# Stick-breaking attention with the queries on the partitions and the suffix sums on VectorE

## What is computed

```
z           = (q @ k.T) * scale                     # per head, queries x keys
past        = s_idx < t_idx
log_beta    = log_sigmoid(z)
log_1mb     = where(past, log_sigmoid(-z), 0)
between     = reverse_cumsum(log_1mb, over keys) - log_1mb
a           = where(past, exp(log_beta + between), 0)
out         = a @ v
```

## Time and profile before

| | us |
|---|---|
| median of 3 runs (1226.33 to 1226.4) | 1226.34 |
| profiled execution | 1226.2 |
| its span | 1224.4 |
| PE busy | 1204.7 (98%) |
| PE weight loads busy | 1053.1 (86%) |
| DVE busy | 772.5 (63%) |
| ACT busy | 609.4 (50%) |
| DMA, bytes moved | 219 MB at 179 GB/s |

### The profile page before, as it was taken

One profiled execution on the slowest core, in us unless ns is written; L12 is line 12 of the kernel. 1 busy time (PEld: TensorE's weight loads), 2 busy tenths in 40 slices (PEclk: granted clock), 3 DMA queues, 4 the chain that ended last, 5 costly groups with the idle time before them and its releaser, 6 DMA issues.

```text
span 1224.4 us, 17707 instructions
## 1 busy us (share of the span) xinstructions
PE 1204.7 (98%) x7176; PEld 1053.1 (86%) x7176; DVE 772.5 (63%) x883; ACT 609.4 (50%) x711; POOL 3.5 (0%) x10
## 2 busy tenths in 40 slices
PE   7999999999999999999999999999999999999997
PEld 6999987888888799899888789999988878899995
DVE  5676966474555665555458687555575868755555
ACT  6565555555444454444257545444435654544441
POOL 0000000000000000000000000000000000000000
PEclk9999999999999999999999999999999999999999
DMA  7654243543655355554364445545436444564540
GB/s 255 207 210 166 104 173 139 205 172 138 218 207 183 126 206 207 176 202 173 135 236 178 147 173 206 207 172 206 171 137 242 168 150 172 199 214 172 206 171 34
DMA packets 34490, 219.25 MB, mean 179 GB/s; under 512 B 4080, under 2 KB 6144, under 8 KB 9088
## 3 DMA queue, kind: packets, MB, share of 16 engines
q1 hardware_dynamic: 33792, 216.31, 49.6%
q0 software_dynamic: 640, 2.11, 0.5%
HBM read 217.34 MB, written 1.06 MB: 178 GB/s over the span
## 4 chain that ended last, share of the span: by engine, by line
PE 92%; DVE 6%; ACT 1%; issue 1%; DMA 0%; SPq 0%; DVEq 0%; ACTq 0%
PE gps L1440 33%; PE gps L1479 9%; PE gps L1487 9%; PE gps L1480 9%; PE aps L1479 7%; PE aps L1480 7%; PE aps L1487 7%; DVE w_lo L788 1%; PE aps L1602 1%; PE aps L1505 1%; DVE rs L919 1%; ACT w_hi L341 1%; DVE B L929 1%; PE aps L1641 1%; DVE B L870 1%
## 5 line engine op out<-in xcount | busy, mean ns | idle before, releaser
L788 DVE TENSOR_TENSOR w_lo<-raw,w_hi 128x2048 fp32r<-128x2048 f32 x194 | 444.2, 2291 | 260.4 <-ACT w_hi L341 259.9
L341 ACT ACTIVATE w_hi<-raw 128x2048 fp32r<-128x2048 f32 x194 | 370.5, 1911 | 208.0 <-PE aps L1487 104.1
L1440 PE MATMUL gps<-R_hi,w_hi 128*128 128x256 f32 x672 | 175.8, 283 | 0.0
L1440 PE MATMUL gps<-R_hi,w_lo 128*128 128x256 f32 x672 | 175.7, 283 | 0.0
L1479 PE MATMUL aps<-w_hi,Q_hi 128*128 128x512 f32 x416 | 162.2, 390 | 0.5 <-DVE Q_lo L1201 0.5
L1480 PE MATMUL aps<-w_lo,Q_hi 128*128 128x512 f32 x416 | 162.2, 390 | 0.0
L1440 PE MATMUL gps<-R_lo,w_hi 128*128 128x256 f32 x672 | 135.4, 283 | 0.0
L1440 PEld LDWEIGHTS gps<-R_hi,w_lo 128*128 128x128 f32 x672 | 128.9, 192 | 0.8
L1440 PEld LDWEIGHTS gps<-R_hi,w_hi 128*128 128x128 f32 x672 | 128.8, 192 | 0.8
L1479 PE MATMUL gps<-w_hi,H_hi 128*128 128x512 f32 x288 | 114.8, 399 | 0.0
L1480 PE MATMUL gps<-w_lo,H_hi 128*128 128x512 f32 x288 | 112.5, 390 | 0.0
(11 more groups left out here) (241 smaller groups left out, 1670.6 us busy)
## 6 DMA issues: line engine op xcount, KB each, us to landing
raw<-w SPq DMA_DIRECT2D x194, 1024.0 KB, 4.8
B<-rows SPq DMA_DIRECT2D x4, 1024.0 KB, 5.6
raw<-w SPq DMA_DIRECT2D x8, 256.0 KB, 6.0
B<-turns POOLq DMA_DIRECT2D x4, 512.0 KB, 7.7
B<-x_t SPq DMA_DIRECT2D x4, 256.0 KB, 5.4
B<-mem_t SPq DMA_DIRECT2D x1, 1024.0 KB, 8.9
B<-x SPq DMA_DIRECT2D x1, 1024.0 KB, 6.8
out<-B SPq DMA_DIRECT2D x4, 256.0 KB, 2.0
```

Source lines behind the costliest of these rows:

```text
L341: act.activation(w_hi[:, ring(l), :], raw[:, raw_slot(l), :], ACT.Copy)\
L788: dve.tensor_tensor(w_lo[:, ring(l), :], raw[:, raw_slot(l), :], w_hi[:, ring(l), :].bitcast(F32), ALU.subtract)\
L1440: return pe.matmul(gps[:, bank_, nt * T:(nt + 1) * T], w[:, r, c:c + P], op[:, k, :], start=start, stop=stop, skip_group_check=True)
```

## The change

The scores are made with the queries on the partitions, with the same numbers of columns. The blocks of a head are now (queries 0, keys 0), (queries 1, keys 0) and (queries 1, keys 1). The suffix sum runs along a row, so it is a backward scan on DVE, one for each head of the pair; the constant `keep` is one except at the last key of each of the two query groups, where it is zero and starts the sum anew. The masks are no longer multiplied in behind softplus and exp. A mask of 0 and -3e38 is added to the two diagonal blocks of the scores as DVE copies them from PSUM to spb, and ACT copies the third block. Softplus works on soft, z stays in spb. The weights come out of exp with queries on the partitions, so PE transposes six blocks of 128x128 per pair and ACT copies them from PSUM to a new tile `sb_pt`, from which the values product reads.

The order changes too. Even slot: PE has values and scores; ACT sb_out, the copy of the third block, a wait for the mask, Abs, Exp, Ln; DVE sb_out and the mask. Odd slot: PE has the transposes of the pair before, behind its half; ACT the copy of the transposed weights of the pair before, then exp; DVE sum, scans and subtraction. The weight splits stand behind this work, in every slot.

```diff
             def sb_softplus(i):
+                b = spb[:, i % 2, :, :]
                 act.wait_ge(s["sb_z"], i + 1)
                 if i >= 2:
-                    act.wait_ge(s["sb_o"], i - 1)
-                b = spb[:, i % 2, :, :]
-                st.mark(act.activation(b, aps[:, 0:2, 0:384], ACT.Abs))
+                    act.wait_ge(s["sb_t"], i - 1)
+                act.activation(b[:, :, 128:256], aps[:, 0:2, 128:256], ACT.Copy).then_inc(s["sb_full"], 1)
+                act.wait_ge(s["sb_past"], i + 1)
+                if i >= 1:
+                    act.wait_ge(s["sb_arg"], i)
+                st.mark(act.activation(soft[:, :, :], b, ACT.Abs))
                 st.settle()
-                st.mark(act.activation(b, b, ACT.Exp, scale=-1.0))
+                st.mark(act.activation(soft[:, :, :], soft[:, :, :], ACT.Exp, scale=-1.0))
                 st.settle()
-                act.activation(b, b, ACT.Ln, bias=one_col).then_inc(s["sb_sp"], 1)
+                act.activation(soft[:, :, :], soft[:, :, :], ACT.Ln, bias=one_col).then_inc(s["sb_sp"], 1)
...
+            def sb_copy(i):
+                act.wait_ge(s["sb_t"], i + 1)
+                if i >= 1:
+                    act.wait_ge(s["sb_o"], i)
+                act.activation(sb_pt, aps[:, 2:4, 0:384], ACT.Copy).then_inc(s["sb_pt"], 1)
...
-                if SB0 <= h <= SB0 + 18 and h % 2 == 0:
+                if SB0 <= h <= SB0 + 18:
                     t = (h - SB0) // 2
-                    if t >= 2:
-                        sb_out(t - 2)
-                    if t < SB_PAIRS:
-                        sb_softplus(t)
-                    if 1 <= t <= SB_PAIRS:
-                        sb_exp(t - 1)
+                    if h % 2 == 0:
+                        if t >= 2:
+                            sb_out(t - 2)
+                        if t < SB_PAIRS:
+                            sb_softplus(t)
+                    elif t < SB_PAIRS:
+                        if t >= 1:
+                            sb_copy(t - 1)
+                        sb_exp(t)
+                    else:
+                        sb_copy(t - 1)
                 if h + 4 < FFN1 + 2:
                     split(0, h + 4)
...
-            def sb_parts(i):
-                b, z = spb[:, i % 2, :, :], aps[:, 0:2, 0:384]
-                dve.wait_ge(s["sb_sp"], i + 1)
-                if i >= 1:
-                    dve.wait_ge(s["sb_t"], i)
-
-                st.mark(dve.scalar_tensor_tensor(soft[:, :, :], z, 0.0, b, ALU.max, ALU.add))
-                st.settle()
-                mask_diagonals(soft, s["sb_soft"])
-
-                dve.scalar_tensor_tensor(b, z, 0.0, b, ALU.min, ALU.subtract).then_inc(s["sb_lb"], 1)
+            def sb_masked(i):
+                b = spb[:, i % 2, :, :].rearrange("p h (c n) -> p h c n", c=3)
+                z = aps[:, 0:2, 0:384].rearrange("p h (c n) -> p h c n", c=3)
+                dve.wait_ge(s["sb_full"], i + 1)
+                if i >= 2:
+                    dve.wait_ge(s["sb_t"], i - 1)
+                dve.tensor_tensor(b[:, :, 0:3:2, :], z[:, :, 0:3:2, :],
+                                  past.unsqueeze(1).unsqueeze(1).to_broadcast([P, 2, 2, P]), ALU.add)\
+                   .then_inc(s["sb_past"], 1)
 
             def sb_arg(i):
                 b = spb[:, i % 2, :, :]
-                dve.wait_ge(s["sb_t"], i + 1)
-                dve.wait_ge(s["sb_lb"], i + 1)
-                dve.tensor_tensor(b, b, aps[:, 2:4, 0:384], ALU.subtract).then_inc(s["sb_arg"], 1)
-
-            def sb_mask(i):
-                dve.wait_ge(s["sb_e"], i + 1)
-                mask_diagonals(spb[:, i % 2, :, :], s["sb_a"])
+                dve.wait_ge(s["sb_sp"], i + 1)
+                dve.scalar_tensor_tensor(soft[:, :, :], b, 0.0, soft[:, :, :], ALU.max, ALU.add)\
+                   .then_inc(s["sb_sum"], 1)
+                dve.wait_ge(s["sb_sum"], i + 1)
+                for hh in range(2):
+                    ins = dve.tensor_tensor_scan(soft[:, hh, ::-1], keep[:, ::-1], soft[:, hh, ::-1], 0.0,
+                                                 ALU.mult, ALU.add)
+                ins.then_inc(s["sb_suffix"], 1)
+                dve.wait_ge(s["sb_suffix"], i + 1)
+                dve.tensor_tensor(b, b, soft[:, :, :], ALU.subtract).then_inc(s["sb_arg"], 1)
...
-                if SB0 <= h <= SB0 + 18 and h % 2 == 0:
+                if SB0 <= h <= SB0 + 18:
                     t = (h - SB0) // 2
-                    if t >= 2:
-                        sb_out(t - 2)
-                    if 1 <= t <= SB_PAIRS:
-                        sb_arg(t - 1)
-                    if t < SB_PAIRS:
-                        sb_parts(t)
-                    if 1 <= t <= SB_PAIRS:
-                        sb_mask(t - 1)
+                    if h % 2 == 0:
+                        if t >= 2:
+                            sb_out(t - 2)
+                        if t < SB_PAIRS:
+                            sb_masked(t)
+                    elif t < SB_PAIRS:
+                        sb_arg(t)
...
             def sb_scores(i):
                 if i >= 1:
-                    pe.wait_ge(s["sb_lb"], i)
+                    pe.wait_ge(s["sb_past"], i)
                 for hh in range(2):
                     q, k = qs[64 * hh:64 * hh + 64, i, :], ks[64 * hh:64 * hh + 64, i, :]
-                    pe.matmul(aps[:, hh, 0:256], k[:, 0:128], q, start=True, stop=True)
-                    ins = pe.matmul(aps[:, hh, 256:384], k[:, 128:256], q[:, 128:256],
-                                    start=True, stop=True)
+                    pe.matmul(aps[:, hh, 0:128], q[:, 0:128], k[:, 0:128], start=True, stop=False,
+                              skip_group_check=True)
+                    ins = pe.matmul(aps[:, hh, 128:384], q[:, 128:256], k, start=False, stop=True,
+                                    skip_group_check=True)
                 ins.then_inc(s["sb_z"], 1)
 
-            def sb_between(i):
-
-                pe.wait_ge(s["sb_soft"], i + 1)
+            def sb_transpose(i):
+
+                pe.wait_ge(s["sb_e"], i + 1)
                 if i >= 1:
-                    pe.wait_ge(s["sb_arg"], i)
+                    pe.wait_ge(s["sb_pt"], i)
                 for hh in range(2):
-                    pe.matmul(aps[:, 2 + hh, 0:384], gt, soft[:, hh, :], start=True, stop=False)
-                    ins = pe.matmul(aps[:, 2 + hh, 128:256], ones, soft[:, hh, 256:384],
-                                    start=False, stop=True)
+                    for j in range(3):
+                        ins = pe.transpose(aps[:, 2 + hh, j * P:(j + 1) * P],
+                                           spb[:, i % 2, hh, j * P:(j + 1) * P], ident)
                 ins.then_inc(s["sb_t"], 1)
 
             def sb_values(i):
-                pe.wait_ge(s["sb_a"], i + 1)
+                pe.wait_ge(s["sb_pt"], i + 1)
...
-                    if 1 <= t <= SB_PAIRS:
-                        sb_between(t - 1)
+                if SB0 + 3 <= h <= SB0 + 17 and h % 2:
+                    sb_transpose((h - SB0 - 3) // 2)
```

More of the change, by code:

```diff
@@ L53 @@
 N_MLP, N_END, N_LN = 0, 1, 2
-C_ID, C_GT, C_LE, C_ONE, C_PAST, CONSTS1 = 0, 128, 256, 384, 512, 640
+C_ID, C_PAST, C_KEEP, C_ONE, CONSTS1 = 0, 128, 256, 384, 640
 C_COS, C_SIN, C_DECAY, C_CAUSAL, CONSTS2 = 0, 128, 384, 1408, 1792
@@ L103, in build @@
         small = sb("small", [P, 4, 16])
-        ident, gt = cst[:, C_ID:C_ID + P], cst[:, C_GT:C_GT + P]
-        le_one = cst[:, C_LE:C_LE + 2 * P]
-        le, ones = cst[:, C_LE:C_LE + P], cst[:, C_ONE:C_ONE + P]
+        ident, ones = cst[:, C_ID:C_ID + P], cst[:, C_ONE:C_ONE + P]
         past = cst[:, C_PAST:C_PAST + P]
+        keep = cst[:, C_KEEP:C_KEEP + 384]
         one_col = cst[:, C_ONE:C_ONE + 1]
@@ L153, in build @@
         bias = B6[:, :, :].rearrange("p h (t k) -> p h t k", t=2)
+        sb_pt = B7[:, 0:3, :].rearrange("p a t -> p (a t)").rearrange("p (h n) -> p h n", h=2)
         fl = spb[:, 0, :, :]
@@ L168, in build @@
             staged_free conv_y cv_hi cv_lo
-            sb_z sb_sp sb_soft sb_lb sb_t sb_arg sb_e sb_a sb_o sb_ohi sb_olo
+            sb_z sb_past sb_full sb_sp sb_sum sb_suffix sb_arg sb_e sb_t sb_pt sb_o sb_ohi sb_olo
             hd_sq hd_var hd_log hd_r hd_z hd_tr hd_out
@@ L1014, in ffn @@
                     split_gates(n)
[L1016 to L1023, removed]
             def sb_out(i):
@@ L1612, in sb_values @@
                     c = (2 * i + hh) * 64
-                    a = spb[:, i % 2, hh, :]
+                    a = sb_pt[:, hh, :]
                     out = gps[64 * hh:64 * hh + 64, 3, :]
@@ L1623, in turn_heads @@
                 if n == 0:
-                    pe.wait_ge(s["sb_lb"], SB_PAIRS)
+                    pe.wait_ge(s["sb_past"], SB_PAIRS)
                 else:
@@ L1950, in shape_constants @@
     c1[:, C_ID:C_ID + P] = np.eye(P)
[L1951 to L1954, removed]
+    c1[:, C_PAST:C_PAST + P] = np.where(i[None, :] < i[:, None], 0.0, -3.0e38)
```

(2 more changed lines are left out.)

## The result

| | before | after |
|---|---|---|
| median, us | 1226.37 (1226.33 to 1226.88, 4 runs) | 1239.01 (1238.7 to 1241.62, 4 runs) |
| profiled execution, us | 1226.2 | 1238.7 |
| span, us | 1224.4 | 1236.9 |
| PE busy, us | 1204.7 | 1203.1 |

A forecast was written before the change was run, and what follows sets the result against it. PE bounds the kernel before; after the change, the ACT-DVE loop makes PE wait. 10.8 - 1.75 + 0.70 + 2.36 + 0.4 = 12.5 us, so 1238.8; main case 1235.5 to 1241 (55%), with rivals 1231 to 1245.

The forecast's parts named there:

- PE's bill: Stick-breaking stage: products removed 1.75 us, transposes added 0.70 a pair, net -1.05; an unhindered pair would take 14.06 us.
- The loop: Stick-breaking stage: closed hand-overs between ACT and DVE, 16.56 us a turn, 16.93 with a convolution slot.
- B: Rival on DVE's scan: it runs at the plain pace, 0.55 us, turn 15.8, total 1232.5 us; chance 12%.
- D: Rival on DVE: mask and scan at their upper ends, turn 16.98, total 1242 us; chance 10%.
- A: Rival, faster: PE stays the bound and gets the full 8.4 us, total 1217.9 us; chance 7%.
- When PE starts to wait: Stick-breaking stage: values 0 just in time at 101.5 us, PE waits 2.4 before values 1, later values follow the loop.
- The long wait: PE waits about 5 us once, ahead of values 6, for ACT's copy behind slot 25's evictions and squares.
- rival C: TensorE's clock falls after PE's 5 us wait: up to +2, 1240.8 us, 10%; low for long, 1246 or more, 3%.
- 2.36 us wait of turn_heads: Slot 27: PE, ready at 210.7 us, waits for head_scale on DVE until 213.0.
- Up to values 6 the loss: Stick-breaking stage: values 6 start at 203.5 us where they stood at 192.7 before, +10.8.

The follow-up runs named there:

- e1: Changed kernel with DVE's sum, scans and subtraction moved to the even slot, ahead of its weight split: 1218.47 us, ratio 0.9937 to the kernel before.
- e5: e1 with every transpose of the attention done twice: 1223.10 us, ratio 0.9976 to the kernel before.
- e4: Changed kernel with every transpose of the attention done twice: 1238.67 us, ratio 1.0097 to the kernel before.
- e3: Changed kernel without the mask on DVE, ACT copying all three score blocks to spb: 1225.96 us, ratio 0.9994 to the kernel before.
- e8: Changed kernel with ACT's weight split ahead of exp in the odd slot, DVE's order kept: 1226.47 us, ratio 1.0007 to the kernel before.
- e2: Changed kernel without the two scans of a pair, sum and subtraction kept: 1225.95 us, ratio 0.9995 to the kernel before.
- e7: e1 with the two scans of a pair done a second time on their own result: 1227.96 us, ratio 1.0016 to the kernel before.
- e6: e1 without the two scans of a pair: 1218.34 us, ratio 0.9933 to the kernel before.

## Why the prediction was right

- **PE's bill.** Removed 1.75, transposes 0.70 a pair. In e1, where nothing else counts, values follow values in 14.0 us against the 14.06 of the sum, and the whole is 7.9 us better than before against 8.4. The transposes have the form and duration taken from the fox stage (271/272/273 ns). Right; the transposes cost 0.65 (e5), so 0.70 was 0.05 too much.
- **The loop and its length.** 16.56 and 16.93 worked out, 16.49 and 16.97 measured. The durations by form, in the changed kernel (ns min/median/max, first and last start):

```profile
L1053 DVE TENSOR_TENSOR_SCAN soft<-cst,soft x16: 931/944/958, 87.0 to 203.9; 128x384 f32<-128x384 f32 x16
...
L494 ACT ACTIVATE soft<-spb x8: 842/846/851, 79.2 to 195.3; 128x768 f32<-128x768 f32 x8
...
L1049 DVE SCALAR_TENSOR_TENSOR soft<-spb,soft x8: 949/950/951, 86.0 to 202.1; 128x768 f32<-128x768 f32 x8
L1057 DVE TENSOR_TENSOR spb<-spb,soft x8: 957/958/958, 88.8 to 204.9; 128x768 f32<-128x768 f32 x8
...
L1610 PE MATMUL aps<-cst,spb x48: 271/272/273, 95.4 to 213.0; 128*128 128x128 f32 x48
...
L1042 DVE TENSOR_TENSOR spb<-aps,cst x8: 678/680/683, 78.5 to 194.6; 128x512 f32<-128x512 f32 x8
```

The scan of 128x384 takes 0.944 us where 0.94 was scaled from one of 8x256; the mask 0.680 for 0.69, Abs 0.846 for 0.84, the sum 0.950 for 0.95. Rivals B and D, which differ in these, are out, and so is A: nothing hid the loop. The page on SBUF and PSUM access (the Trainium skill, Perfetto Trace Analysis, Optimizing Scalar/DVE Operations) is not borne out for DVE: the sum reads SBUF alone and takes 0.950, where the sum before read one operand from PSUM and took 0.95; Abs went from 0.81 to 0.846, as the page has it for ScalarE.
- **When PE starts to wait.** Values start at 101.92, 117.63, 134.12, 151.10, 168.07 and 184.56 us, where 101.5, 117.9, 134.5, 151.4, 168.4 and 185.0 were forecast: from the second on each 0.3 to 0.4 early. The waits of PE are 1.62, 2.41, 1.39, 2.88 and 1.15 us, where 2.4 to 2.9 each were forecast. What a turn loses is its length less the 14.0 that PE needs: 1.7, 2.5, 3.0, 3.0 and 2.5. The first, second and fourth wait agree with that within 0.1. The first is short because values 0 came 0.4 late and values 1 0.3 early. The third and the fifth are 1.6 and 1.3 short, and in just these two turns the granted clock was down at the start (0.50 in 136 to 138 and in 170 to 172 us): PE worked more slowly and arrived later, so the wait is shorter and the turn is not longer.
- **The long wait.** Its size was right and its place was not. It was forecast ahead of values 6, for the copy. It is in the middle of half 26, whose second bank is the one that slot 25 must evict, and ACT reaches that eviction only behind the split of half 28, which it does in slot 24. The bank is free at about 200.3 and the copy ready at 203.2, and PE needs 2.7 us at full speed for the second part of the half, so by either path values 6 would start near 203.4: the sum hides the mistake.
- **The clock (rival C).** It came, and cost little. Stretches of the changed kernel (from:to and length in us; busy us and instructions of PE, PEld, DVE, ACT and POOL; the granted clock; the DMA share; GB/s):

```profile
196.00:198.00 2.00, 0.00 (x0) 0.00 (x0) 0.00 (x0) 1.94 (x4) 0.00 (x0) 1.00 0.84 328
198.00:200.00 2.00, 0.00 (x0) 0.00 (x0) 0.15 (x1) 2.00 (x3) 0.00 (x0) 0.92 0.34 143
200.00:202.00 2.00, 1.65 (x4) 1.36 (x5) 2.00 (x1) 1.97 (x8) 0.00 (x0) 0.50 0.00 0
...
206.00:208.00 2.00, 2.00 (x13) 1.38 (x12) 0.00 (x0) 2.00 (x2) 0.00 (x0) 0.88 0.23 94
```

PE's timeline of the same kernel, its first matmuls after the wait:

```profile
200.35 0.80 PE L1485 MATMUL gps<-w_hi,R_hi 128*128 128x512 f32 x1 [4.97 <-ACT sqh L357]
...
201.37 0.63 PE L1485 MATMUL gps<-w_hi,R_hi 128*128 128x512 f32 x1
```

PE has stood idle since 195.4 (200.35 less 4.97). The granted clock falls near 199.8 to half, which is the 1.2 GHz level (mean 0.50 in 200 to 202), and is full again, 2.4 GHz, from about 206.5. The matmuls from 201.37 are 0.43 us apart and not 0.23. The twelve from 200.35 to the end of the half lose about 0.20 each, 2.4, and values 6 start at 205.84, where 203.5 was forecast. But turn_heads behind them was to wait 2.4 us for head_scale in any case. It starts at 213.14, 0.1 us after the forecast 213.0, without a wait. DVE's last scalings ahead of it:

```profile
211.35 1.14 DVE L1072 TENSOR_SCALAR sqh<-sqh,small 128x256 f32<-128x256 f32 x4
```

They end at 212.49, so with a full clock turn_heads could have started at about 212.5. The clock then costs some 0.6 us of the 2.4 at the end (an estimate from these rows). The clock also falls, for shorter times, at two of the waits under 3 us (0.84 in 130 to 137, 0.89 in 162 to 171 us); there PE ran into the next wait anyway. All this is argued from the trace, and not shown by a run. The runs give this much: in e4 a mean clock of 0.997 goes with 1237.8 and 1238.1 us, one of 0.993 or 0.994 with 1239.3 and 1239.2, so up to 1.3 us may belong to it there; the four runs of the changed kernel (0.992 to 0.995) show no such order, the longest, 1241.62, has the highest clock. So a price of about 0.6 us, up to 1, is likely and not shown.

What was left to chance: the sum met the time within 0.3 us, and that is closer than its terms. Up to values 6 the loss is 13.05 us (205.84 against 192.79), not 10.8, because of the clock; the 2.36 us wait of turn_heads is nothing, because PE came late to it. These two cancel for a reason: head_scale, which hangs on the loop, sets the end whichever of them happens. That head_scale ended 0.5 us ahead of the forecast and the clock then cost 0.6 is luck. The runs of one changed kernel here spread over 1.5 to 6.8 us, so the last tenths of the agreement mean nothing.

## What to carry to other kernels

When work moves from the bound engine to two others, sum up what they do, but then also walk their queues: if each waits for the other several times per period, the length of that closed walk is a bound of its own, and it can be exceeded with both engines half idle. In each queue, put the work that another engine waits for ahead of the work that nobody needs soon, and put what has to wait for another engine behind it. Here one move of four instructions in DVE's order was worth 20.5 us and turned a loss of 12.6 us into a gain of 7.9.

## What the runs showed that was not expected

The profiled executions of e3 and e8 are 5.3 and 1.3 us above what was expected, and part of that comes from another stage. In the fox stage of the second block one weight half comes late in every kernel; how late differs. The row of ACT's split that waits for it, in the timeline of the kernel before:

```profile
641.71 1.91 ACT L341 ACTIVATE w_hi<-raw 128x2048 fp32r<-128x2048 f32 x1 [5.02 <-DMA raw<-w]
```

The same row in e1:

```profile
634.37 1.92 ACT L341 ACTIVATE w_hi<-raw 128x2048 fp32r<-128x2048 f32 x1 [6.09 <-DMA raw<-w]
```

And the wait of PE that follows it in e1:

```profile
PE aps L1811 <- DVE spb L1312: 1.4, 1, 1.4
```

Where that split waits 5.0 to 5.9 us for its load (before, after, e2, e4, e5, e7), PE does not wait in the fox transposes, or by 0.3 us at most. Where it waits 6.1 to 6.4, PE waits 1.4 us there (e1), 1.5 (e8), 2.1 (e6) and 2.3 (e3). So 2.3 of the 5.3 us of e3 come from there; where the rest comes from is open. How much of the spread of the runs comes from there is not shown: only profiled executions have a trace. The load is issued when DVE's split has freed its raw buffer. From the end of that split to the start of ACT's it is 6.9 us in the kernel before, 7.4 in e1 and 8.1 in e3, so it is the load's own time that differs. Two other loads of 512 KB each (B<-turns) are under way in the same stretch; whether they cause it was not tried.
